# First loads and fills of a recurrence moved into the attention, an attention combine split over VectorE and GpSimd, a rounding order changed

## The reference

```python
m_t = jnp.maximum(inter, jnp.max(dmat, axis=-1))
qk = jnp.einsum('ntd,nsd->nts', qq, kk) * jnp.exp(dmat - m_t[:, :, None])
num = w_inter[..., None] * jnp.einsum('nvd,ntd->ntv', C, qq) + jnp.einsum('nts,nsv->ntv', qk, vv)
den = w_inter * jnp.einsum('nd,ntd->nt', n, qq) + qk.sum(-1)
h = num / jnp.maximum(jnp.abs(den), jnp.exp(-m_t))[..., None]
C_new = a[:, None, None] * C + jnp.einsum('ns,nsv,nsd->nvd', w, vv, kk)
```

```python
s = jnp.einsum('bqhmd,bkhmd->bhmqk', q_blk, k) * scale + bias[None, :, None]
p = jax.nn.softmax(s, axis=-1)
w = p[:, :, 0] - lam * p[:, :, 1]
return jnp.einsum('bhqk,bkhe->bqhe', w.astype(v.dtype), v)
```

## Time and profile before

| | |
|---|---|
| runs | 2845.3, 2840.91, 2833.8 us (median 2840.91) |
| profiled execution, its own time | 2843.98 us |
| span of its profile | 2842.2 us |
| mean granted TensorE clock | 0.979 |
| TensorE products busy (PE) | 2704.3 us, 95% |
| TensorE weight loads busy (PEld) | 2248.8 us, 79% |
| VectorE busy (DVE) | 1551.3 us, 55% |
| ScalarE busy (ACT) | 990.6 us, 35% |
| GpSimd busy (POOL) | 314.1 us, 11% |
| DMA | 248.67 MB, mean 87 GB/s |

### The profile page before, as it was taken

The page is one execution under the profiler, slowest core; times in us unless marked ns, Lnnn a source line. Parts: engine busy times, 40 slices in busy tenths (PEclk is TensorE's granted clock), DMA queues, the critical chain, the costliest instruction groups (busy, mean ns, idle before and its releaser), DMA issues. The chain is left out here.

```text
span 2842.2 us, 38333 instructions
## 1 busy us (share of the span) xinstructions
PE 2704.3 (95%) x15464; PEld 2248.8 (79%) x15464; DVE 1551.3 (55%) x2466; ACT 990.6 (35%) x1846; POOL 314.1 (11%) x273
## 2 busy tenths in 40 slices
PE   6999999999999999999989989998999999999998
PEld 4789888878866798888878778755688888888886
DVE  4312565777644514757766546779644444444445
ACT  3201233655522311335645334378522211211112
POOL 0000100332431001102214400000100000000001
PEclk8999999999999999999989999989999999999999
DMA  6322222116465223321163421100401110110111
GB/s 273 103 81 81 78 83 83 24 35 227 141 236 209 85 75 82 95 74 46 32 215 116 163 96 55 45 1 1 156 1 34 56 59 30 59 59 30 59 50 76
DMA packets 135894, 248.67 MB, mean 87 GB/s; under 512 B 27106, under 2 KB 90260, under 8 KB 127936
## 3 DMA queue, kind: packets, MB, share of 16 engines
q1 hardware_dynamic: 114592, 231.83, 24.4%
q10 hardware_dynamic: 21152, 14.75, 1.6%
HBM read 198.24 MB, written 43.05 MB: 85 GB/s over the span
## 5 line engine op out<-in xcount | busy, mean ns | idle before, releaser
L967 PE MATMUL ps<-xn_hi_sb,ft_hi_sb 128*128 128x512 f32 (+1 forms) x720 | 263.4, 366 | 1.0 <-DVE ft_lo_sb L1423 1.0
L968 PE MATMUL ps<-xn_lo_sb,ft_hi_sb 128*128 128x512 f32 (+1 forms) x720 | 262.9, 365 | 0.0
L969 PE MATMUL ps<-xn_hi_sb,ft_lo_sb 128*128 128x512 f32 (+1 forms) x720 | 262.9, 365 | 0.0
L3160 DVE TENSOR_TENSOR arena_sb<-arena_sb,ps 128x512 f32<-128x512 f32 x256 | 173.0, 686 | 121.4 <-PE ps L2843 118.5
L919 PE MATMUL ps<-tm_hi_sb,xn_hi_sb 128*128 128x512 f32 (+2 forms) x608 | 216.3, 356 | 16.6 <-DVE xn_lo_sb L1337 8.2
L921 PE MATMUL ps<-tm_hi_sb,xn_lo_sb 128*128 128x512 f32 (+2 forms) x608 | 213.7, 351 | 0.0
L920 PE MATMUL ps<-tm_lo_sb,xn_hi_sb 128*128 128x512 f32 (+2 forms) x608 | 213.4, 351 | 0.0
L2802 PE MATMUL ps<-xn_hi_sb,w_up_hi_sb 128*128 128x512 f32 x512 | 199.4, 389 | 0.0
L2804 PE MATMUL ps<-xn_hi_sb,w_up_lo_sb 128*128 128x512 f32 x512 | 199.2, 389 | 0.0
L2803 PE MATMUL ps<-xn_lo_sb,w_up_hi_sb 128*128 128x512 f32 x512 | 199.2, 389 | 0.0
L2841 PE MATMUL ps<-w_down_hi_sb,h_hi_sb 128*128 128x512 f32 x480 | 186.7, 389 | 0.0
(11 more groups left out here) (422 smaller groups left out, 6113.5 us busy)
## 6 DMA issues: line engine op xcount, KB each, us to landing
arena_sb<-in_w_ft SPq DMA_DIRECT2D x44, 512.0 KB, 3.6
arena_sb<-mqk_dram SPq DMA_DIRECT2D x36, 512.0 KB, 3.3
arena_sb<-x_dram SPq DMA_DIRECT2D x33, 512.0 KB, 6.9
arena_sb<-in_w_ada SPq DMA_DIRECT2D x16, 1024.0 KB, 9.1
arena_sb<-in_w_up SPq DMA_DIRECT2D x16, 1024.0 KB, 6.6
arena_sb<-in_w_down SPq DMA_DIRECT2D x16, 1024.0 KB, 4.9
arena_sb<-in_xall SPq DMA_DIRECT2D x20, 512.0 KB, 4.9
arena_sb<-mv_dram SPq DMA_DIRECT2D x40, 256.0 KB, 4.0
```

Of the source, the lines that this page charges most:

```text
L967: pe.matmul(to, hi, xn_hi_flat[:, k, at:at + size], start=k == 0, stop=False)
L968: pe.matmul(to, hi, xn_lo_flat[:, k, at:at + size], start=False, stop=False)
L969: mm = pe.matmul(to, lo, xn_hi_flat[:, k, at:at + size], start=False, stop=k == KT - 1)
```

## The change

It has four parts.

1. **Rounding order at the start** (layer 0, ScalarE). Pieces 0 and 1, first half of the activations, piece 2, second half, piece 3, in place of four pieces and then both halves.
2. **First loads in the attention** (both layers, SP). The loads of steps 0 and 1 are asked for in the attention after block b = 2, behind waits for the stores of the projections. The load of `w_out` goes out at j = 1 in layer 0, as before, and at j = 3 in layer 1.
3. **Front beside the last division** (both layers). TensorE waits for `m_init` and `a_out` in `back` of half-step 0 and no longer ahead of the first front. VectorE fills the ones columns in block 1 of the attention, behind a wait for stores that used that memory, and the state ahead of the last division.
4. **The combine in two** (second block). VectorE (`ratio`) multiplies map 1 in place by the ratio, with one tensor operand, and GpSimd (`combine`) adds it to map 0 in two halves, for the first 30 steps; VectorE does the last two by itself, in halves. Map 0 has three buffers and map 1 two. TensorE's `turn_p` comes in halves, `values` in quarters, in another order, and ScalarE's `attended` comes ahead of `evacuate`.

```diff
-        prob2 = [[part(W2 + 2048 * u + 1024 * m, SEQ) for m in range(2)] for u in range(2)]
+        prob2 = [[part(W2 + at, SEQ) for at in (0, 2048, 4096)], [part(W2 + at, SEQ) for at in (1024, 3072)]]
...
+                        if b == 2:
+                            mlstm_first(l)
...
+                def mlstm_first(l):
                     for u in range(4):
                         sp.wait_ge(tm_out[u], 16 * ((TM_ALL - u + 3) // 4))
                     for u in range(2):
                         sp.wait_ge(mqk_out[u], 16 * 4)
...
+                        if j < 2:
+                            load_state(j, tiles, outputs)
...
+                def mlstm(l):
+                    nt = layer_tiles(l)
+                    sp.wait_ge(a_out[l], nt)
...
+                        if j >= 2:
+                            load_state(j, tiles, outputs)
+                        if j == (1 if nt > NX else 3):
                             sp.dma_start(w_out, A["w_out"][l]).then_inc(p_w[l], 16)
...
                 def mlstm(l):
                     nt = layer_tiles(l)
-                    pe.wait_ge(a_out[l], nt)
-                    pe.wait_ge(m_init[l], 1)
...
+                        if n == 0:
+                            pe.wait_ge(m_init[l], 1)
+                            pe.wait_ge(a_out[l], nt)
...
+                            if b == 1 and h == 1:
+                                for slot in range(2):
+                                    dve.wait_ge(ft_az_st[l][slot], 32)
+                                for d in range(2):
+                                    for slot in range(2):
+                                        dve.memset(mv_ring[d][slot][:, :, MD:MD + 1], 1.0)
...
                     gate_out(last, last % 2)
+                    dve.memset(c_state, 0.0).then_inc(m_init[l], 1)
                     divide(last)
...
-                        for n in range(4):
-                            high_piece(n)
-                        high(l, 0)
+                        high_piece(0)
+                        high_piece(1)
+                        high_half(l, 0, 0)
+                        high_piece(2)
+                        high_half(l, 0, 1)
+                        high_piece(3)
...
-                sp.wait_ge(d_t, 4 * NX)
+                sp.wait_ge(d_t, 8 * NX)
...
+                            of, p, at = (b, 0, 2 * h - 4) if h >= 2 else (b - 1, 1, 2 * h)
+                            if h % 2 and of >= 0:
+                                values(of, p, at)
+                            turn_p(s, h, 0)
+                            if h % 2 == 0 and of >= 0:
+                                values(of, p, at)
+                            if of >= 0:
+                                values(of, p, at + 1)
                             if more:
                                 scores(*following, 1)
-                            if h >= 2:
-                                values(b, 0, h - 2)
-                            elif not first:
-                                values(b - 1, 1, h)
+                            turn_p(s, h, 1)
...
+                        dve.tensor_scalar(row_max[:, u, h:h + 1], l_all[:, s // 4, 2 * h:2 * h + 1], neg_lam[:, :], c, ALU.mult, ALU.mult).then_inc(d_ratio, 1)
+                        p0, p1 = prob2[0][s % 3], prob2[1][s % 2]
+                        dve.wait_ge(d_ratio, min(2 * s, BY_POOL + s) + 1)
+                        if s < BY_POOL:
+                            dve.tensor_scalar(p1, p1, row_max[:, u, h:h + 1], None, ALU.mult).then_inc(d_ratio, 1)
+                            return
...
+                        if m == 0 and s >= 3:
+                            act.wait_ge(d_t, 2 * (s - 2))
+                        if m == 1 and s >= 2:
+                            act.wait_ge(d_w, 2 * (s - 1))
...
+                def combine(s):
+
+                    pool.wait_ge(d_ratio, 2 * s + 2)
+                    p0, p1 = prob2[0][s % 3], prob2[1][s % 2]
+                    for half in range(2):
+                        at = slice(SEQ // 2 * half, SEQ // 2 * (half + 1))
+                        pool.tensor_tensor(p0[:, at], p0[:, at], p1[:, at], ALU.add).then_inc(d_w, 1)
...
+                for s in range(BY_POOL):
+                    combine(s)
```

More of the change, by code:

```diff
@@ L2631, in scores, with turn_p, values @@
                         mm.then_inc(d_s[m], 1)
-                    def turn_p(s, h):
-                        pe.wait_ge(d_w, s + 1)
-                        if not isinstance(s, int) or s > 0:
+                    def turn_p(s, h, half):
+                        pe.wait_ge(d_w, 2 * s + half + 1)
+                        if half == 0 and s > 0:
                             pe.wait_ge(d_t_act, s)
-                        for n in range(NX):
-                            mm = pe.transpose(ps[:, 4 + n // 4, (n % 4) * P:(n % 4 + 1) * P], prob2[h % 2][0][:, n * P:(n + 1) * P], ident[:, :])
+                        for n in range(4 * half, 4 * half + 4):
+                            mm = pe.transpose(ps[:, 4 + half, (n % 4) * P:(n % 4 + 1) * P], prob2[0][s % 3][:, n * P:(n + 1) * P], ident[:, :])
                         mm.then_inc(d_t, 1)
-                    def values(b, p, half):
-                        if half == 0:
+                    def values(b, p, quarter):
+                        if quarter == 0:
                             pe.wait_ge(d_t_act, 4 * b + 2 * p + 2)
@@ L2646, in values @@
                                 pe.wait_ge(d_y, b)
-                        for n in range(4 * half, 4 * half + 4):
+                        for n in range(2 * quarter, 2 * quarter + 2):
                             for g in range(2):
@@ L2651, in values @@
                                                start=n == 0, stop=n == NX - 1)
-                        if half == 1:
+                        if quarter == 3:
                             mm.then_inc(d_pv, 1)
@@ L2689, in attention @@
                         group_mean(dw_acc, j, mu_mm)
-                    for half in range(2):
-                        values(NX - 1, 1, half)
+                    for quarter in range(4):
+                        values(NX - 1, 1, quarter)
                 def group_mean(src, n, done):
@@ L3022, in query_block @@
                             last = isinstance(b, int) and b == NX - 1
-                            combine(s, u, h)
+                            ratio(s, u, h)
                             if h < 3 or not last:
@@ L3359, in query_block @@
                                 exp(s + 2, *((u, h + 2) if h < 2 else (1 - u, h - 2)), 0)
+                            if h == 1 and b > 0:
+                                attended(b - 1)
                             evacuate(s, h)
@@ L3365, in query_block @@
                                 queries(4 + s)
-                            if h == 1 and b > 0:
-                                attended(b - 1)
                     act.wait_ge(sub_ready, 1)
```

55 lines of the change are left out of this document (23 added, 32 removed).

## The result

| | before | after |
|---|---|---|
| median of 7 runs | 2840.91 us | 2826.29 us |
| lowest and highest | 2833.8 to 2848.63 | 2823.04 to 2830.99 |
| profiled execution, its own time | 2843.98 us | 2829.66 us |
| span of its profile | 2842.2 us | 2827.4 us |
| mean granted TensorE clock | 0.979 | 0.979 |

The ratio is 0.9949, with a 95% interval of 0.9937 to 0.9962: 14.6 us less by the medians. The forecast was 19.4 us less, 2821.5.

A forecast was written before the change was run, and what follows sets the result against it. TensorE works nearly all the time, so edits pay only where it waits or another engine paces it. Terms 2.0 + 2.0 + 7.5 + 7.9 = 19.4 us, from 2843.98 to 2824.6, 2821.5 as a median; range 2813 to 2829.

The forecast's parts named there:

- the time of the first product, 42.05: Start, layer 0: TensorE's first product at 42.05 in place of 44.05, after a rounding subtraction of 1.23 us; 2.0 us.
- The gain up to half-step 8: Second layer's recurrence: earlier front, no 6.44 us wait at half-step 4 and no cooling behind it; 9.9 us.
- The hand-over and the context half-steps: Second layer: fill ahead of the division lets ScalarE's key weighting start 1.9 us early, and the context half-steps keep it.
- the two half-steps behind the stall: Second layer's recurrence: they take 11.40 us against 9.76 for two later ones, so cooling costs 1.6 us more.
- the new wait: Second layer, half-step 8, loads behind the 4 MB: 0 to 2.2 us, taken as 1.5, plus 0.9 for a slower clock.
- rival (b): Second layer: the stall only moves, half-step 8 waits 6.4 us and TensorE cools; part 3 brings 2 to 3; 2826.5; 12%.
- the sign of (b): Second layer's recurrence, profile after: a wait above 4 us at half-step 8, where 0 to 2 us was forecast.
- The layout by hand: Second block's attention, two steps: 3.61 + 4.01 us, taken as 3.85 each against 4.15; TensorE stands 0.6 us in even ones.
- Rival (a): Second block's attention: the hand-over through GpSimd eats part 4, leaving 1.5 us of it; 2828; 13%.
- rival (c): Second block's attention: VectorE and GpSimd hold each other's port, halves cost 2.15 us, 25 us lost; 2854.5; 4%.
- All behind it moves along: Behind the second block's attention: folds and output weights come earlier too, so the 7.9 us of part 4 is kept.
- the new combine misses it: Second block's attention: VectorE's multiply starts 0.26 us behind GpSimd's last half, and the maxima read PSUM, so no lock.

The follow-up runs named there:

- e2: Changed kernel with the second layer's 4 MB of output weights loaded in eight 512 KB pieces, one behind each half-step's loads from 6 to 13: 2820.41 us, ratio 0.9929.
- e11: Changed kernel with the second layer's output weights in eight pieces and the early front beside the last division undone: 2823.14 us, ratio 0.9929.
- e5: Kernel before with only the second block's combine split between VectorE and GpSimd: 2833.75 us over 12 runs, ratio 0.9979.
- e3: Changed kernel with the early front undone: TensorE waits again for the last division and fills; early loads and later output weights stay: 2828.23 us, ratio 0.9962.
- e1: Changed kernel with the second layer's 4 MB of output weights asked for at step 1 again, ahead of half-step 4's loads: 2830.37 us, ratio 0.996.
- e7: Changed kernel with GpSimd adding the whole map in one operation in place of two halves: 2848.69 us, ratio 1.0026.
- e4: Changed kernel with the second block's attention as before, VectorE combining the two maps alone in one operation: 2828.45 us, ratio 0.9951.
- e8: Changed kernel with one wait added: GpSimd casts the second block's output weights only after VectorE's twelve folds: 2817.53 us, ratio 0.9918.
- e10: Changed kernel with each of GpSimd's two casts of the second block's output weights made in eight 128x512 operations: 2824.45 us, ratio 0.9931.
- e12: Changed kernel with output weights in eight pieces, VectorE's multiply in halves and GpSimd's casts behind the folds: 2812.53 us, ratio 0.9895.

## Why the prediction was right, point by point

The time fell inside the range, on the side that was forecast, and 4.8 us above the likeliest value. Of the four terms parts 1 and 4 were right for the reasons given. Part 3 came out near its number by errors that cancel, and nothing in the sum stood for what was lost behind part 4.

**Part 1** was put at 2.0 us. One pair of profiles gives 1.66 at the first product and 1.75 at 240, the means over all profiles 1.6. The step that was 0.3 too good is the time of the first product, 42.05: VectorE's low part followed at 42.39.

**Part 2** was put at 2.0 us, and the pair of profiles shows 1.56. TensorE's clock was at 1.2 GHz for 10.2 us from 642.3 on, before for 6.8 around there. At equal length of the fall (e2 against e11) it is 2.5. The ten profiles with the new hand-over stand 1.6 to 3.5 ahead of before from 630 to 665, 2.4 in the mean, and e5, with the old one, 2.0 behind it, so the 2.0 is borne out in size and not closer. The early loads and the moved fills cost nothing that could be seen.

**Part 3** was put at 7.5 us and measured 7.03, but by two errors that cancel. The gain up to half-step 8 was 13.2 us (from a drift of -0.79 at 1400 to -14.0), not 9.9. The hand-over and the context half-steps won 3.1, not 1.9, and 0.6 came just before. And the two half-steps behind the stall were compared with two later ones, 9.76 us. The right comparison is what they take when they don't follow a stall: 3.09 + 5.19 = 8.28, since half-step 5's front finds TensorE free. So the stall and its cooling cost 3.1 us more than the wait, not 1.6. On the other side the new wait was 4.29 us, with 1.9 for cooling, not 1.5 and 0.9. The failing step is the size of that wait. The 4 MB were asked for at 1438.96 and half-step 8 was wanted at 1452.9, a gap of 14.0 us where the forecast had 14.9. And its values landed 18.3 us behind the issue of the 4 MB, beyond both bounds of 14.9 and 17.1. In the six other profiles with this code it is 18.1 to 19.0 us, and the wait 4.1 to 5.3. Half-step 7's loads, asked for 0.9 us ahead of the 4 MB, do not explain it by themselves: in e3 they stand just as far ahead, and the values land after 17.1. What sets the landing stays open. So rival (b), the stall that only moves, was nearer in its mechanism than the 12% it had: a wait of two thirds of the old one came back, above the 4 us that the prediction named as the sign of (b). Its price of 2 to 3 us for the part didn't follow, because what stands ahead of it won more. e1 and e2 show both ends of the order: 5.1 us worse and 6.0 better. That this pair of profiles shows 7.03 for a forecast of 7.5 is partly luck: the same code gives 5.3 to 8.5 from profile to profile.

**Part 4** was put at 7.9 us. The pair of profiles shows 8.04 and the comparison at equal clock 7.9. The layout by hand held nearly to the number: plain steps 3.67 and 4.04 us in turn (forecast 3.61 and 4.01, taken as 3.85), 3.851 on average; query steps 4.58 (4.65 forecast); TensorE's wait in even steps 0.72 (0.6); GpSimd's halves 1.274 us (1.276). Rival (a) is ruled out by these rows and e5, rival (c) by the halves. What e7 adds is that (a) was near: with one addition in place of two halves the attention takes 165.0 us from the first scores to the last combine, and the old one (e4) 145.7.

The step that failed here is a sentence, "All behind it moves along". Behind the attention TensorE waited 1.67 us at the end of the chain of VectorE's folds, and TensorE's own work came earlier in relation to them, so that it waits 2.43 now. That alone costs nothing, but the longer wait is followed by a fall of the clock in 5 of the 9 profiles with the new attention and the cast in its old place, and in neither of the 2 with the old attention. Each fall costs 1.6 us. That is the 1.61 in the table. The counts alone do not show that the longer wait brings the fall. It fits that none of the three kernels without the long wait (e8, e10, e12) has one. The trace of before held the row for it, the wait of 1.67 us, and the 4.08 us of the fold that makes it.

**The rest**, from 18.4 - 1.6 = 16.8 us down to the 14.8 of the two profiles, is the places that no part touches, 3.08 + 1.71 - 1.64 = 3.15 lost, and 1.2 won in small drifts. The medians of seven runs each differ by 14.6; the interval of the ratio holds 10.8 to 17.9 us, so that the 16.8 is inside it and 19.4 not.

**The port pair.** The Trainium skill, "SBUF — State Buffer", section "SBUF: two separate sides", makes the port pair of VectorE and GpSimd an exclusive lock. The prediction argued that the new combine misses it, and it did: 60 halves between 1.261 and 1.283 us. The lock shows elsewhere, with a price: a fold of 0.69 us took 4.08 beside a cast of 3.76 us (the rows in e8), and with the cast in pieces three folds took 1.09 (e10). The trace agrees that it is held for an operation.

## What to carry to other kernels

When a large load stands ahead of small ones on a queue, moving it moves the stall: cut it into pieces that fit in the slack behind each small load; here the stall went. Work handed from VectorE to GpSimd and on to TensorE paid here only because TensorE got the first part early (e7); lay two steps out by hand before building, since the odd and the even one have different limits. After a stage has been made faster, look at the first wait behind it: here a longer one was followed by a fall of TensorE's clock in 5 of 9 profiles.

## What was not expected of the hardware

A two-tensor VectorE operation on SBUF of 0.69 us took 4.08 us beside a GpSimd cast of 128x4096, in all profiles where the cast stood there, and it lay on the path of TensorE: one added wait (e8) won 4.0 us, 2.4 where no fall of the clock was in it. Beside pieces of 128x512 the folds took 1.09 us and the pieces 1.07 instead of 0.61, so the two alternate. VectorE's operations of 128x512 with one operand in PSUM did not suffer from GpSimd's second cast (0.75 us each).

The same happens in the recurrence, in the kernel before too, and nothing here takes it away. The prediction read the 2.332 us of the earlier trace rows as a single case. The trace of before has four: two on L1697 (2.33) and two on the next operation, L1699 (2.29), each beside one of GpSimd's subtractions for the low parts of the output weights, 128x1024, 2.36 us. The second layer's first one in the changed kernel, with GpSimd's pair of subtractions, VectorE's operation and TensorE's wait:

```profile
1475.87 4.70 POOL L2323 TENSOR_TENSOR w_out_lo_sb<-w_out_raw_sb,w_out_hi_sb 128x1024 fp32r<-128x1024 f32 x2 [7.40 <-ACT w_out_hi_sb L2105]
...
1478.24 2.35 DVE L1713 SCALAR_TENSOR_TENSOR den_sb<-den_sb 128x4 f32<-128x4 f32 x1
...
1482.43 0.46 PE L1147 MATMUL ps<-arena_sb 128*128 128x129 f32 x2 [1.60 <-ACT arena_sb L2100]
```

TensorE waits 1.6 to 1.7 us behind each, and the next front comes 6.7 to 6.8 us after the one before it in place of 4.88. That is some 7 us a run, an estimate from these gaps which no run tests.

The clock falls at places that the code doesn't fix: near 800 in 4 of 14 profiles and near 1245 in 5, for 3.4 to 6.8 us, at 1.6 to 3.1 us each. The first steps of the attention ran at a mean granted clock between 0.63 and 0.89, and took 31.2 to 36.3 us with the same instructions. Differences of under 5 us between whole times of this kernel say little without the stages.
